# Sums of squares in the two last layers: GpSimd adds six of eight blocks, and the second sum stands earlier

## The reference, cut to what matters

```
def rms_norm_2(x, g):
    xf = x.astype(jnp.float32)
    y = xf * lax.rsqrt(jnp.mean(xf * xf, axis=-1, keepdims=True) + EPS)
    return (y * g.astype(jnp.float32)).astype(x.dtype)

    for l in range(DEPTH_2):
        h = rms_norm_2(x, attn_norm_g[l])
        proj = h @ w_in[l]
        ...
        x = x + merged @ w_out[l]
        hf = rms_norm_2(x, ffn_norm_g[l])
        u = depthwise_conv(hf @ ffn_w_up[l], ffn_conv_w[l], ffn_conv_b[l])
        u_gate, u_val = u[..., :D_FF], u[..., D_FF:]
        x = x + (jax.nn.silu(u_gate) * u_val) @ ffn_w_down[l]
```

## Time and profile before

| | us |
|---|---|
| median of 3 runs | 2156.4 |
| lowest and highest | 2155.51, 2159.56 |
| the profiled execution | 2156.41 |
| its span (first to last instruction) | 2154.6 |
| TensorE busy | 2047.8 |
| VectorE busy | 893.4 |
| ScalarE busy | 628.6 |
| GpSimd busy | 31.1 |

### The profile page before, as it was taken

How to read it: one execution, slowest core, us unless ns; L and a number is a source line. 1 busy time by engine, 2 the same in 40 slices (tenths; PEclk the granted TensorE clock), 3 DMA queues, 4 the chain that set the end, 5 groups by cost and what they waited for, 6 DMA issues and landing times.

```text
span 2154.6 us, 31774 instructions
## 1 busy us (share of the span) xinstructions
PE 2047.8 (95%) x12318; PEld 1314.1 (61%) x12319; DVE 893.4 (41%) x1608; ACT 628.6 (29%) x967; POOL 31.1 (1%) x45
## 2 busy tenths in 40 slices
PE   6998999999999999999999999999999999999999
PEld 4863333333333333333333598879999888789999
DVE  2522221112212221122122346866885348766874
ACT  1422111111111111111111225443654144634553
POOL 0000000000000000000000020000000020000000
PEclk9998999999999999999999999999999999999999
DMA  9786999399999999999499564413654554334563
GB/s 345 268 328 265 393 417 402 134 417 417 417 419 418 417 417 418 419 418 417 179 371 417 217 195 128 147 55 103 203 189 158 140 158 132 111 99 145 171 204 108
DMA packets 222040, 580.36 MB, mean 269 GB/s; under 512 B 23520, under 2 KB 142048, under 8 KB 185984
## 3 DMA queue, kind: packets, MB, share of 16 engines
q1 hardware_dynamic: 221952, 579.09, 70.7%
HBM read 577.74 MB, written 1.31 MB: 269 GB/s over the span
## 4 chain that ended last, share of the span: by engine, by line
PE 69%; DMA 11%; SPq 8%; DVE 6%; ACT 3%; issue 3%; ACTq 0%; DVEq 0%
PE bank L1080 13%; DMA ring<-in_w_gu 9%; PE bank L1136 8%; PE bank L807 6%; SPq L680 4%; SPq L682 4%; PE bank L1424 3%; PE bank L1425 3%; PE bank L1426 3%; PE bank L1032 3%; PE bank L1046 3%; PE bank L1211 2%; PE bank L877 2%; PE bank L1213 2%; PE bank L1212 2%
## 5 line engine op out<-in xcount | busy, mean ns | idle before, releaser
L1080 PE MATMUL bank<-ring,heap 128*64 128x512 f32 x2176 | 494.6, 603 | 30.4 <-DMA ring<-in_w_gu 30.4
L1080 PEld LDWEIGHTS bank<-ring,heap 128*64 128x64 f32 x2176 | 149.0, 138 | 359.2 <-issue 266.0
L2045 DVE TENSOR_SCALAR heap<-bank 128x256 f32<-128x256 f32 (+1 forms) x72 | 26.7, 412 | 725.2 <-PE bank L1080 696.5
L1136 PE MATMUL bank<-ring,heap 128*64 128x512 f32 (+1 forms) x1152 | 255.1, 595 | 0.0
L1424 PE MATMUL bank<-h_hi,w_hi 128*128 128x256 f32 x640 | 181.7, 284 | 3.4 <-DVE w_lo L2321 3.4
L2321 DVE TENSOR_TENSOR w_lo<-ring,w_hi 128x2048 fp32r<-128x2048 f32 (+1 forms) x64 | 142.4, 2226 | 97.6 <-ACT w_hi L1739 97.6
L1425 PE MATMUL bank<-h_lo,w_hi 128*128 128x256 f32 x640 | 181.1, 283 | 0.0
L1426 PE MATMUL bank<-h_hi,w_lo 128*128 128x256 f32 x640 | 181.1, 283 | 0.0
L1575 ACT ACT_TABLE_LOAD x32 | 41.1, 1283 | 471.8 <-DVE heap L2045 470.2
L1136 PEld LDWEIGHTS bank<-ring,heap 128*64 128x64 f32 (+1 forms) x1152 | 78.7, 135 | 150.7 <-issue 145.0
L1739 ACT ACTIVATE w_hi<-ring 128x2048 fp32r<-128x2048 f32 (+1 forms) x64 | 119.1, 1860 | 145.4 <-PE bank L1426 85.9
(11 more groups left out here) (336 smaller groups left out, 3065.3 us busy)
## 6 DMA issues: line engine op xcount, KB each, us to landing
ring<-in_w_gu SPq DMA_DIRECT2D x256, 1024.0 KB, 19.1
ring<-in_w_down SPq DMA_DIRECT2D x128, 1024.0 KB, 21.4
ring<-in_ffn_w_up SPq DMA_DIRECT2D x44, 1024.0 KB, 7.7
ring<-in_w_in SPq DMA_DIRECT2D x32, 1024.0 KB, 5.6
ring<-in_w_ada SPq DMA_DIRECT2D x24, 1024.0 KB, 10.8
ring<-in_ffn_w_down SPq DMA_DIRECT2D x16, 1024.0 KB, 6.7
ring<-in_w_out SPq DMA_DIRECT2D x8, 1024.0 KB, 4.9
ring<-in_w_in SPq DMA_DIRECT2D x3, 2048.0 KB, 27.1
```

The costliest lines, as they stand in the source:

```text
L1080: last = mm(psum[g][both[f], :], xgT[:, k % 4, k // 4, :], wt[:, g, :, :, f, :].rearrange("p i c n -> p (i c) n"), start=False, stop=k == ...
L1136: last = mm(psum[2][FEW * f:FEW * f + n, :], hidT[:, o:o + n], wt[:, 512 * f:512 * (f + 1)], start=k == 0, stop=k == DT - 1)
```

## The change

```
-LCH = {"dve": 125, "pool": 19}
+LCH = {"dve": 125, "pool": 23}
...
                     if k == DT - 3:
                         done("sq1", 4)
-                        product(ss1[:, 0:T], lambda k: const("ones"), lambda k: L["sq"][:, k, :], DT).then_inc(lay_full.sem, 1)
+                        done("fold", 1)
+                        product(ss1[:, 0:T], lambda k: const("ones"), lambda k: L["sq"][:, (0, 6, 7)[k], :], 3) \
+                            .then_inc(lay_full.sem, 1)
...
                 ss2 = lay("ss2")
                 b = halves(lay("up0"))
-                plain(b, 0, range(6))
-                for k in range(DT):
-                    if k % 2 == 0:
-                        done("sq2", k // 2 + 1)
-                    last = mm(ss2[:, 0:T], const("ones"), L["sq"][:, k, :], start=k == 0, stop=k == DT - 1)
+                plain(b, 0, range(4))
+                done("fold", 2)
+                mm(ss2[:, 0:T], const("ones"), L["sq"][:, 0, :], start=True, stop=False)
+                done("sq2", 4)
+                for k in (6, 7):
+                    last = mm(ss2[:, 0:T], const("ones"), L["sq"][:, k, :], start=False, stop=k == 7)
                 last.then_inc(lay_full.sem, 1)
-                plain(b, 0, range(6, DT)).then_inc(lay_full.sem, 1)
+                plain(b, 0, range(4, DT)).then_inc(lay_full.sem, 1)
...
+                def fold(sig):
+
+                    q = L["sq"]
+                    for i in (1, 2):
+                        pool.wait_ge(S[sig].sem, S[sig].at(i + 1, l))
+                        c.step(g.tensor_tensor(q[:, 0:2, :], q[:, 0:2, :], q[:, 2 * i:2 * i + 2, :], ALU.add))
+                    g.tensor_tensor(q[:, 0, :], q[:, 0, :], q[:, 1, :], ALU.add).then_inc(S["fold"].sem, 1)
+
+                fold("sq1")
                 pool.wait_ge(S["vecs"].sem, S["vecs"].at(1, l))
...
+                fold("sq2")
                 assert c.n == LCH["pool"], ("pool", c.n)
```

More of the change, by code:

```diff
@@ L537, in build @@
             "ksq": 1, "kvar": 2, "kstd": 1, "kn": 1, "rope_m": 3, "krope": 1, "mixed": 1,
-            "nmax": 2 * NH, "pexp": 2 * NH, "pnorm": 2 * NH, "merged": 4, "sq2": 4, "var2": 1, "std2": 1,
+            "nmax": 2 * NH, "fold": 2, "pnorm": 2 * NH, "merged": 4, "sq2": 4, "var2": 1, "std2": 1,
             "h2": 2, "vals": FT, "conv": FT, "silu": FT, "ffact": FT,
```

## The result

In the first comparison the changed kernel took 2143.36 us (median of 4 executions, 2142.3 to 2145.38) beside 2155.95 for the kernel before (4 executions on the same chip, 2155.22 to 2159.56). The ratio is 0.9941, with an interval from 0.9927 to 0.9955: 12.6 us less, where 8.3 were forecast. The profiled execution took 2143.75, its span is 2142.0.

What follows compares the result with a forecast made beforehand. TensorE's queue was taken as the bound, except at the second norms, where VectorE, ScalarE and weight landings count. Gains of 1.2 + 2.2 + 2.7 + 2.2 = 8.3 us took 2156.4 to 2148.1; range 2145.0 to 2151.8.

Steps and rivals of the forecast that it cites:

- Price of a product: TensorE's products with ones at all four norms: 0.431 us each, so five fewer save 2.16 us per place.
- An addition of 128x512: GpSimd's additions of squares: 1.28 us each, twice the 0.64 of a 128x256 one, with ends 0.64 and 2.57.
- Second norm, first layer: Mean starts 3.15 us earlier, but the `up2` weights then hold `leading(4)`: gain 2.7 us.
- Second norm, second layer: Weights landing after 8.4 us already hold `leading(4)`: gain 2.16 + 0.1, taken as 2.2 us.
- First norm, second layer: GpSimd's additions are covered by 10 us and VectorE idles until the sum: gain 2.16 us, summed as 2.2.
- First norm, first layer: 2.16 us saved, less 0.9 where GpSimd's addition holds up VectorE: net gain 1.2 us.
- The term of 0.9 for the block: First layer's first norm: GpSimd's first addition makes VectorE's L2086 stand 0.9 us; ends 0 and 1.9.
- from the sum to the range: Whole kernel: ends 2145.8 and 2151.5 us, a little wider for the spread of runs: 2145.0 to 2151.8.
- No block: First layer's first norm: GpSimd doesn't get between VectorE's instructions or L2086 isn't held; 2147.2 us, chance 18%.
- `up2` not sooner: Second norms: `up3` close behind shares the engines, `up2` lands when it did, both give nothing; 2153.0 us, chance 12%.
- Given back in the attention: Attention: a VectorE and ScalarE stretch doesn't move with TensorE, the first norms' 3.4 us go; 2151.5 us, chance 9%.
- Fold late: At the sums TensorE waits for GpSimd's additions, should they take far longer; slower, 2158.6 us, chance 4%.

Runs made afterwards that it cites:

- `first_only`: Changed kernel with GpSimd's additions at the two first norms alone, the second norms as before the change: 2152.39 us, ratio 0.9982 to the kernel before.
- `second_only`: Changed kernel with GpSimd's additions and the earlier sum at the two second norms alone, first norms as before: 2151.57 us, ratio 0.9982 to the kernel before.
- `fold_in_place`: Changed kernel with the second norms' sum back after six blocks of up0 instead of four: 2147.51 us, ratio 0.9965 to the kernel before.
- GpSimd later: Changed kernel with GpSimd's first addition waiting for the fourth square in the first layer's first norm; run twice: 2142.94 and 2142.28 us.
- the order alone: Kernel before with the second norms' eight-product sum after four blocks of up0 instead of six, no GpSimd additions: 2154.81 us, ratio 0.9994.
- the slow fold: Changed kernel with ten more 128x256 GpSimd additions ahead of the last one at each second norm: 2157.92 us, ratio 1.0016 to the kernel before.

## Why the prediction was wrong

**The mechanisms held.** TensorE's queue is what sets the first norms; the second norms end in `leading(4)`, held by the landing of `up2`. GpSimd's work is covered at all four places. No wait for GpSimd came in; the idle time before the mean went; TensorE still waits at unit 4. `first_only`, `second_only` and `fold_in_place` each gave at their places what the sum says of them, but for the second layer, where both norms gave 0.4 to 0.5 us more (below).

**The terms, in order:**

- *Price of a product*: 2.16 for five. Measured 2.16 and 2.18 (the fold without the order) and 2.20 (GpSimd later). Right.
- *An addition of 128x512*: 1.28 forecast, 1.27 to 1.29 measured where nothing held it, 1.56 and 2.88 beside VectorE. Right.
- *Second norm, first layer*: 2.7 forecast; 2.73, 2.50, 2.70. The mean came 3.24 sooner (3.15 forecast), and its weights were late next, as the step says. Right.
- *Second norm, second layer*: 2.2 forecast; 2.73, 2.44, 2.60. The step took the landing of 8.4 us in the first trace of before for a property of this place. In after it was 7.9 in both layers. The landing differs from execution to execution, and the two second norms are alike: 0.4 too little. The step's own sum then holds everywhere: 2.16, plus 0.6, less what the landing takes over 7.85, gives each of the twelve gains of the second norms with fold and order to 0.02 us (2.73 for a landing after 7.88, 2.44 for one after 8.17), and without the 2.16 it gives the order alone as well (-0.87 for 9.32, 0.24 for 8.21).
- *First norm, second layer*: 2.2 forecast; 2.29, 2.42, 2.62. What exceeds 2.16 is not the change's. Ahead of `cq` TensorE waits for the weights of this layer, and the first trace of before had the longest of these waits, 1.90; the others of before and the kernels without the fold there had 0.94 to 1.49, and are ahead of it by just that difference (0.96 to 0.42). With the difference of the waits taken off, all eight traces with the fold there give 2.16 to 2.17. Right. Timelines of before and of the kernel with the order alone:

```profile
1687.38 5.45 PE L1232 MATMUL bank<-heap,ring 128*128 128x256 f32 x24 [1.90 <-DMA ring<-in_w_in]
```

```profile
1687.85 5.45 PE L1232 MATMUL bank<-heap,ring 128*128 128x256 f32 x24 [0.94 <-DMA ring<-in_w_in]
```

- *First norm, first layer*: 1.2 forecast; 1.58 three times. The block was there and of the kind forecast (0.96 instead of 0.35 for L2086, the L2089 of after). The addition ended 0.81 us after VectorE's step had begun, and the step took 0.61 longer; the two steps held later took 1.04 and 0.54 longer, with 1.24 and 0.73 of the addition left, and the place did not lose by them. The term of 0.9 for the block was mis-sized: it was 0.6, shown by the run that takes it away (1.58 to 2.20). The Trainium skill (SBUF — State Buffer, section Who interferes with whom) says that whoever issues first has the shared ports for its whole instruction and the other is blocked. The trace agrees for these three steps in that the step ended only behind the addition; the price is some 0.2 us less than what is left of GpSimd's instruction. For the step at 1214.87, which by the profile's starts began behind the addition and was not held, it does not agree; no run shows in which order the two were issued.

Together the places give 1.58 + 2.16 + 2.64 + 2.59 = 9.0 us (means of the three traces, 2.16 for the first norm of the second layer). Forecast 8.3.

**The step that failed** is the last one: from the sum to the range. I said that the profiled execution and the median may be exchanged, took the ends of the four places, and widened them a little for the spread of three runs. What executions differ by outside the places stood in the sum at nothing; in the first trace of after it is 3.4 us, 2.0 at the start and 1.5 for one low-clock stretch. What the traces show beside the places is larger than their ends. There are stretches at the low clock, about 1.5 us of cost each, which one execution of a kernel has and another of the same kernel lacks. Sixteen executions of the changed kernel have a mean of 2145.28 (standard error 0.92), 10.4 less than before, and a median of 2144.70, 0.3 below the range's low end; the first four happened to lie at 12.6. The single profile of before that I read had the latest start of all and the longest wait for the second layer's weights.

Of those 10.4 the places explain 9.0. The mean granted clock of the changed kernel was 0.98756 where it was 0.98675 before. An estimate from that, at the most, since it takes TensorE to be on the path throughout: 0.0008 x 2150 = 1.7 us more at full speed, and 9.0 + 1.7 = 10.7. The later GpSimd does likewise: 9.7 for its places, a clock of 0.98870, which is 0.0019 x 2150 = 4.2, together 13.9; measured 13.4. Over the 72 executions of the kernel before, time and mean clock correlate with -0.72, so the clock is a large part of what makes executions differ. For the other kernels the sum is within about 1 us, the size of its error, and there the clock term does not make it better: fold without order 8.1 by the places and 6.9 with the clock, measured 7.7; `first_only` 3.7 and 4.7, measured 3.5 (4.3 by the span); `second_only` 5.3 and 4.9, measured 4.0 (4.5).

**What stays open** is whether the change raises the mean clock, or whether these executions happened to have it. For the changed kernel the 1.7 us are within two standard errors (1.1 each). For the kernel with the later GpSimd the 4.2 are five of them (0.8), so there it is hardly chance, and no run shows what in the edit it comes from. The shorter wait at unit 4 (1.1 instead of 1.7) is not what does it: in all twelve traces no low-clock stretch follows a wait of 1.07 to 1.71 there, 22 in number, and one follows each of the two longer ones, which had a late landing in front of them.

**The rivals.** *No block*: refuted for the change as made, and then made true by starting GpSimd later. *`up2` not sooner*: refuted, it was issued sooner by as much as TensorE was. With the order alone it is issued when it was, as the change of order alone implies. *Given back in the attention*: refuted, the ledger there is flat except for the low-clock stretch, in after's favour. *Fold late*: did not occur; the slow fold shows its price and that it would have been slower.

## What to carry to other kernels

Follow a gain past the first wait that it removes: the sum two steps sooner moved the mean by 1.73 us and could give no more than 0.6 of it, since the weights behind it come when TensorE's queue lets them, and less whenever they land late. Work for a second engine is free when its inputs lie ready in time and it runs where VectorE idles. Beside VectorE's short instructions its price here was 0.2 us less than the part of its instruction that was left when they wanted to start, and a later start took it away. For a change of under 1% take the spread of many executions into the range, and read the effect from the places in more than one trace, as the span of one can be off by several us.

## What the runs showed of the hardware

- The low clock (0.50, 1.2 GHz) came behind all four waits of TensorE of over 2.5 us in the layers (2.57, 2.79, 4.47 and 4.48). It came behind 15 of the 24 waits of 1.47 us in the attention, which are the same in every trace, behind none of the 22 waits of 1.07 to 1.71 at unit 4, and near 1305 and 1770 in most traces behind no wait of over 0.5. So the wait alone does not decide it. A stretch more or less in the layers moved the end by about 1.5 us; all traces had 10 to 27 us of low clock there.
- The second DMA of `up2` landed after 7.8 to 8.4 us in 22 of 24 cases (two in each trace), and after 9.3 and 9.5 in the other two.
- A GpSimd addition and VectorE's instructions held each other up in both directions: 0.35 became 0.96, 0.88 and 1.39 on VectorE, and 1.28 became 2.88 on GpSimd:

```profile
1472.61 2.88 POOL L2417 TENSOR_TENSOR heap<-heap 128x512 f32<-128x512 f32 x1 [183.12 <-ACT heap L1735]
...
1477.36 1.29 POOL L2417 TENSOR_TENSOR heap<-heap 128x512 f32<-128x512 f32 x1 [1.87 <-ACT heap L1735]
```
